# Four waits reordered, and the low parts of C and S moved from GpSimd to VectorE in three blocks of a hybrid decoder layer

## The reference

```
u, z, xbc, dt = split(rms_norm(h) @ w_in)
xbc = silu(causal_conv4(xbc));  x, B, C per group (4 groups, 6 heads of 64, state 128)
for each chunk of 128 positions, each group:
    y_diag = ((C B^T) * decay, causal) @ (x * dt)
    y_off  = (C @ S) * exp(a_cs)
    S      = S * exp(a_sum) + B^T @ (x * dt * decay_to_end)
    y      = rms_norm_group((y_diag + y_off + d_skip * x) * silu(z)) * ssm_norm_w
h = h + concat(pool_scale * (pooled(u) @ pool_w), y) @ w_out
h = h + relu(rms_norm(h) @ w_ff1)^2 @ w_ff2
```

## Time and profile before

| | |
|---|---|
| median of 3 runs | 2731.99 us (2728.07 to 2734.66) |
| profiled execution | 2732.35 us, its span 2730.6 us |
| TensorE busy | 2688.2 us, 98% |
| VectorE, ScalarE, GpSimd busy | 60%, 47%, 40% |
| mean granted clock of TensorE | 0.996 of 2.4 GHz |

### The profile page before, as it was taken

One profiled execution on the slowest core, in us unless ns is written; L12 is line 12 of the kernel. 1 busy time (PEld: TensorE's weight loads), 2 busy tenths in 40 slices (PEclk: granted clock), 3 DMA queues, 4 the chain that ended last, 5 costly groups with the idle time before them and its releaser, 6 DMA issues. The chain is left out here.

```text
span 2730.6 us, 37588 instructions
## 1 busy us (share of the span) xinstructions
PE 2688.2 (98%) x14034; PEld 2251.3 (82%) x14034; DVE 1629.4 (60%) x2193; ACT 1279.8 (47%) x2562; POOL 1078.9 (40%) x858
## 2 busy tenths in 40 slices
PE   8999999999999999999999999999999999999998
PEld 6788777988788987888988888888888888888887
DVE  3588722678426775158764466664444666666666
ACT  2476754557325665246642554554545322222323
POOL 1033331234101333013334588765555535353434
PEclk9999999999999999999999999999999999999999
DMA  9677586545556446555356546673444843333323
GB/s 292 214 264 251 188 289 239 211 175 189 214 199 236 153 176 228 206 224 187 147 211 242 177 162 228 246 277 131 167 144 175 329 155 107 140 110 137 116 93 154
DMA packets 225491, 531.14 MB, mean 195 GB/s; under 512 B 14090, under 2 KB 98062, under 8 KB 215838
## 3 DMA queue, kind: packets, MB, share of 16 engines
q1 hardware_dynamic: 225310, 528.74, 54.0%
HBM read 382.74 MB, written 145.95 MB: 194 GB/s over the span
## 5 line engine op out<-in xcount | busy, mean ns | idle before, releaser
L1785 PE MATMUL bank<-hnT_hi,w_ring 128*128 128x512 f32 x1152 | 369.3, 392 | 0.7 <-DMA w_ring<-w_scr 0.7
L2129 PE MATMUL bank<-w_first,T_hi 128*128 128x512 f32 x896 | 275.9, 389 | 0.1
L2248 DVE SCALAR_TENSOR_TENSOR acc<-pre,par,acc 128x512 f32<-128x512 f32 x240 | 212.0, 883 | 91.8 <-ACT pre L1304 85.9
L1785 PEld LDWEIGHTS bank<-hnT_hi,w_ring 128*128 128x128 f32 x1152 | 216.3, 188 | 45.4 <-issue 1.0
L2595 DVE TENSOR_TENSOR acc_th<-bank,acc_th 128x512 f32<-128x512 f32 x224 | 150.0, 686 | 155.9 <-PE bank L2129 155.7
L2097 PE MATMUL bank<-T_hi,w_both 128*128 128x512 f32 x768 | 242.2, 389 | 0.2 <-DVE ff L2536 0.2
L1829 PE MATMUL bank<-w_ring,T_hi 128*128 128x512 f32 x768 | 240.2, 394 | 0.0
L1785 PE MATMUL bank<-hnT_lo,w_ring 128*128 128x512 f32 x576 | 224.5, 390 | 0.0
L2129 PEld LDWEIGHTS bank<-w_first,T_hi 128*128 128x128 f32 x896 | 168.1, 188 | 35.4 <-issue 0.5
L1809 PE MATMUL bank<-w_ring,hnT_hi 128*128 128x384 f32 x768 | 195.9, 336 | 0.0
L1785 PE MATMUL bank<-hnT_hi,w_both 128*128 128x512 f32 x576 | 193.0, 407 | 2.1 <-DVE w_both L540 2.1
(11 more groups left out here) (308 smaller groups left out, 6234.9 us busy)
## 6 DMA issues: line engine op xcount, KB each, us to landing
w_ring<-w_scr SPq DMA_DIRECT2D x312, 512.0 KB, 4.2
T_scr<-stage SPq DMA_DIRECT2D x32, 1792.0 KB, 6.6
w_scr<-w_both SPq DMA_DIRECT2D x104, 512.0 KB, 4.0
pair_raw<-in_w_ff SPq DMA_DIRECT2D x36, 1024.0 KB, 5.5
third<-T_scr SPq DMA_DIRECT2D x28, 1024.0 KB, 4.9
pair_raw<-T_scr SPq DMA_DIRECT2D x28, 1024.0 KB, 4.8
sums<-sums_scr SPq DMA_DIRECT2D x64, 384.0 KB, 4.9
raw<-in_w_in SPq DMA_DIRECT2D x36, 512.0 KB, 5.9
```

Source lines behind the costliest of these rows:

```text
L1785: mm = nc.tensor.matmul(bank[s][:, :], w[:, k, :], t[:, k, :], start=(k == 0 and j == 0), stop=(k == KT - 1 and j == 2))
L2129: mm = nc.tensor.matmul(bank[4 * half + t][:, :], a[:, k, tok], w[:, k, :], start=(SECOND[q % 7] not in GOES_ON and k == 0 and j == 0), st ...
L2248: ins = nc.vector.scalar_tensor_tensor(acc[:, s, 0:TB], pre[:, s, k:k + TB], w, acc[:, s, 0:TB], ALU.mult, ALU.add)
```

## The change

1. **Output weights** (`scale_rows`, `high_part`): the scaling of unit N + 1 is done in the call of high_part(N), ahead of N's waits for the unit before and for the store (from unit 38 on; units 36 to 38 are scaled in their own call, now ahead of the other waits). The copies T_hi of the pool mixer move from u = 0, 1 to u = 1, 2.
2. **Sums' store**: in block 0 behind load(12) and no longer behind load(11).
3. **z of step 12**: in block 0 the three transposes of z, with their wait for the units, move from slot1 to behind the unit n2 and get a semaphore of their own; ScalarE's copy moves behind its evacuation of that unit; the mask waits for C B^T alone.
4. **Offset copies**: in steps 14 and 15 of every block, the finish of the pool unit moves behind yo.
5. **Low parts of C and S** in blocks 1 to 3: two subtractions leave GpSimd's queue and become `cs_low` in VectorE's, behind xw and ahead of y_low.

```diff
@@ -25,6 +25,7 @@
 KT = D_MODEL // P
 CONV_TILES = (D_SSM + 2 * GROUPS * P) // P
 STEPS = GROUPS * CH
+Z_LATE = STEPS - CH
 
 
 UNITS_G = 8
@@ -352,6 +353,7 @@
                        for c in range(CH)]
         xb_ps = sig("xb_ps", STEPS)
         zc_ps = sig("zc_ps", STEPS)
+        z_late = sem("z_late")
         xb_ready = sig("xb_ready", STEPS)
         exp_ready = sig("exp_ready", STEPS)
         zs_ready = sig("zs_ready", STEPS)
@@ -506,6 +508,9 @@
 
         def scale_rows(act, N):
 
+            if not U_OUT <= N < UNITS:
+                return
+            act.wait_ge(raw_ready[N % RING], 16 * (N // RING + 1 + (N % RING == 0)))
             if N in FOLDED:
                 f = FOLDED.index(N)
                 for kk in range(2):
@@ -523,9 +528,11 @@
 
             if N >= UNITS:
                 return
+            if U_OUT <= N <= U_OUT + 2:
+                scale_rows(act, N)
+            if N >= U_OUT + 2:
+                scale_rows(act, N + 1)
             act.wait_ge(raw_ready[N % RING], 16 * (N // RING + 1 + (N % RING == 0)))
-            if N >= U_OUT:
-                scale_rows(act, N)
             if N >= 2:
                 act.wait_ge(unit_done.sem, N - 1)
                 act.wait_ge(w_stored[N % 2], 32 * (N // 2))
@@ -794,7 +801,7 @@
                     N0 = b * UNITS
                     for n in range(RING, U_OUT):
                         load(N0 + n, in_unit(n))
-                        if n == (8 if b else 11):
+                        if n == (8 if b else 12):
                             store_sums(b)
                         if n == (8 if b else 12):
                             sums_stored.wait(sp, b, 16 * GROUPS)
@@ -1071,15 +1078,6 @@
                         if b and n == 0:
                             inverse_root(b - 1, r2[:, :], ssf[:, :], h_sumsq, CH, h_rstd, CH)
                     for q, g, c, n1, n2 in mixer_plan(b):
-                        if b:
-                            cs_split_hi.wait(pool, b, 2 * q + 1)
-                            nc.gpsimd.tensor_tensor(c_both[:, 1, :],
-                                                    group_tile(g, 1)[:, c * P:(c + 1) * P],
-                                                    c_both[:, 0, :].bitcast(F32), ALU.subtract)
-                            cs_split_hi.wait(pool, b, 2 * q + 2)
-                            nc.gpsimd.tensor_tensor(s_both[:, 1, :], S[:, g, :],
-                                                    s_both[:, 0, :].bitcast(F32), ALU.subtract
-                                                    ).then_inc(s_split_lo.sem, 1)
                         if q:
                             inverse_root(b, rsy[:, :], ssy[:, :], ssy_ready, q, rsy_ready, 1)
 
@@ -1391,6 +1389,15 @@
                     rsy_ready.wait(act, b, q + 1)
                     nc.scalar.activation(y[:, :], y[:, :], ACT.Copy, scale=rsy
                                          ).then_inc(yn_ready.sem, 1)
+
+                def z_copy(q):
+                    if q == Z_LATE:
+                        act.wait_ge(z_late, 1)
+                    else:
+                        zc_ps.wait(act, 0, q + 1)
+                    gated.wait(act, 0, q)
+                    nc.scalar.activation(zs[:, :], bank[3][:, 0:GW], ACT.Copy
+                                         ).then_inc(zs_ready.sem, 1)
 
                 def y_squares(b, q):
                     gated.wait(act, b, q + 1)
@@ -1483,11 +1490,8 @@
                                              ).then_inc(xb_ready.sem, 1)
                         if b and n1 is None:
                             s_high(b, q)
-                        if b == 0:
-                            zc_ps.wait(act, b, q + 1)
-                            gated.wait(act, b, q)
-                            nc.scalar.activation(zs[:, :], bank[3][:, 0:GW], ACT.Copy
-                                                 ).then_inc(zs_ready.sem, 1)
+                        if b == 0 and q != Z_LATE:
+                            z_copy(q)
                         if q:
                             y_squares(b, q - 1)
                         if q > 1:
@@ -1503,6 +1507,8 @@
                             high_part(act, N0 + n2[0] + 2)
                         for n in n2:
                             evac(b, n)
+                        if b == 0 and q == Z_LATE:
+                            z_copy(q)
                         pending = n2[-1]
                     y_squares(b, STEPS - 1)
                     y_high(b, STEPS - 2)
@@ -1513,8 +1519,8 @@
                             high_part(act, N0 + U_OUT + d * 8 + u + 2)
                             if d == 0 and u == 0:
                                 y_norm(b, STEPS - 1)
-                            if d == 0 and u < 2:
-                                for i in (2 * u, 2 * u + 1):
+                            if d == 0 and u in (1, 2):
+                                for i in (2 * u - 2, 2 * u - 1):
                                     up_out.wait(act, b, pool_item(b) + i + 1)
                                     nc.scalar.activation(T_hi[:, i, :], F[:, i * TB:(i + 1) * TB],
                                                          ACT.Copy).then_inc(pool_hi.sem, 1)
@@ -1849,6 +1855,17 @@
                                                  h[:, t, k * P:(k + 1) * P], ident[:, :])
                     mm.then_inc(hT_ps.sem, 1)
 
+                def z_transposes(q, g, c):
+
+                    zs_ready.wait(pe, 0, q)
+                    if c == 0:
+                        up_out.wait(pe, 0, (g + 1) * UNITS_G)
+                    for i in range(3):
+                        mm = nc.tensor.transpose(bank[3][:, i * P:(i + 1) * P],
+                                                 group_tile(g, 5 + i)[:, c * P:(c + 1) * P],
+                                                 ident[:, :])
+                    return mm
+
                 def slot1(b, q, g, c):
 
                     cols = slice(c * P, (c + 1) * P)
@@ -1865,13 +1882,8 @@
                                                  group_tile(g, j)[:, cols], ident[:, :])
                     mm.then_inc(xb_ps.sem, 1)
                     g_ready.wait(pe, b, q)
-                    if b == 0:
-                        zs_ready.wait(pe, b, q)
-                        if c == 0:
-                            up_out.wait(pe, b, (g + 1) * UNITS_G)
-                        for i in range(3):
-                            nc.tensor.transpose(bank[3][:, i * P:(i + 1) * P],
-                                                group_tile(g, 5 + i)[:, cols], ident[:, :])
+                    if b == 0 and q != Z_LATE:
+                        z_transposes(q, g, c)
                     nc.tensor.matmul(bank[3][:, GW:GW + P], group_tile(g, 0)[:, cols],
                                      group_tile(g, 1)[:, cols], start=True, stop=True
                                      ).then_inc(zc_ps.sem, 1)
@@ -2011,6 +2023,9 @@
                             state(b, q - 1)
                         for n in n2:
                             unit(b, n)
+                        if b == 0 and q == Z_LATE:
+                            g_ready.wait(pe, b, q + 1)
+                            z_transposes(q, g, c).then_inc(z_late, 1)
                         y_offset(b, q, g, c)
                     y_transposes(b, STEPS - 2)
                     diagonal(b, STEPS - 1)
@@ -2333,6 +2348,14 @@
                     scd_ready.wait(dve, b, q + 1)
                     nc.vector.tensor_tensor(S[:, g, :], bank[7][:, 0:GW], S[:, g, :], ALU.add
                                             ).then_inc(state_ready.sem, 1)
+
+                def cs_low(b, q, g, c):
+                    cs_split_hi.wait(dve, b, 2 * q + 2)
+                    nc.vector.tensor_tensor(c_both[:, 1, :], group_tile(g, 1)[:, c * P:(c + 1) * P],
+                                            c_both[:, 0, :].bitcast(F32), ALU.subtract)
+                    nc.vector.tensor_tensor(s_both[:, 1, :], S[:, g, :],
+                                            s_both[:, 0, :].bitcast(F32), ALU.subtract
+                                            ).then_inc(s_split_lo.sem, 1)
 
                 def xw_low(b, q):
                     xw_split_hi.wait(dve, b, q + 1)
@@ -2441,6 +2464,8 @@
                         nc.vector.tensor_tensor(by_head(xw[:, :]), by_head(xb[:, :]),
                                                 per_head(dtw, c, g), ALU.mult
                                                 ).then_inc(xw_ready.sem, 1)
+                        if b:
+                            cs_low(b, q, g, c)
                         if q > 1:
                             y_low(b, q - 2)
                         if b:
@@ -2448,15 +2473,14 @@
                         if c and n1 is not None:
                             finish(b, pending)
                         finish(b, n1)
-                        if n1 is None and c >= 2:
-                            finish(b, pending - 1)
-
                         yoff_ps.wait(dve, b, q + 1)
```

(2 more changed lines are left out.)

## The result

The changed kernel takes 2762.72 us (median of 4 runs, 2760.14 to 2764.26) and the kernel before, on the same chip, 2732.82 us (2728.07 to 2734.66). The ratio is 1.011, with a 95% interval of 1.0096 to 1.0123: slower by 29.9 us. The forecast was 2768.5 us with a range of 2746 to 2785. The profiled span is 2761.2 us against 2730.6.

A forecast was written before the change was run, and what follows sets the result against it. The prediction took TensorE's work plus its waits (busy 2688.2 of 2730.6 us) as the bound. From 2732.35 us, less 17.6 of gains, plus 44.6 of y_offset waits and 9.2 of slow clock: 2768.5 us, range 2746 to 2785.

The forecast's parts named there:

- The chain of 5.90 us: Blocks 1 to 3: uncontended time from the start of state_add through xw and the low parts to y_offset, 5.90 us.
- The sign that the taps take 2.3 us everywhere: VectorE's three taps: with GpSimd's subtraction gone they take 2.3 us everywhere in the new trace.
- The waits: Blocks 1 to 3: y_offset waits 1.13, 2.43 and 1.40 us in steps like 1, 2 and 4; 44.6 us in all.
- The meeting: GpSimd's ty meets VectorE's low-part subtractions: 0.5 us in steps like 1 and 2, 0.25 us in those like 4.
- The clock: Nine y_offset waits of about 2.4 us slow TensorE's clock, costing 9 x 0.6 x 1.7 = 9.2 us.
- The share of 0.6: The factor 0.6 applied to nine long y_offset waits, each slow-clock stretch costing 1.7 us.
- Block 0: Gains in block 0: sums' store 3.8 us, z of step 12 2.0 us, output weights 2.8 us.
- Offset copies: Steps 14 and 15: waits for yo go, net 8.8 - 3.2 = 5.6 us, plus 3.4 us of slow clock.
- Rival 1: Blocks 1 to 3: meetings with GpSimd cost nothing and the clock drops once at most; 2748 us, chance 0.20.
- Rival 2: Meetings cost 0.83 us in 18 steps, all nine long waits halve the clock, gains 14 us; 2785.6 us, chance 0.12.
- Rival 3: VectorE reaches cs_low in time, so the gains alone remain; 2714.8 us, chance 0.03.
- rival 4: The named stalls go but the costs happen to cancel them; 2732 us, chance 0.03.

The follow-up runs named there:

- e5: The changed kernel with GpSimd's product ty moved behind its carry in blocks 1 to 3: 2749.78 us.
- e3: The changed kernel with the subtractions of C and S ahead of the mask in steps 0 to 11, between xdt and xw in 12 to 15: 2714.88 us.
- e2: The kernel before with only the low parts of C and S moved to VectorE behind xw: 2778.77 us.
- e6: The kernel before with only the output weights' scaling and the pool copies T_hi moved: 2729.58 us.
- e7: The kernel before with only the sums' store moved one load later in block 0: 2730.53 us.
- e8: The kernel before with only the finish of the pool units moved behind yo in steps 14 and 15: 2724.38 us.
- e10: The kernel before with only the late z transposes of step 12 in block 0: 2728.78 us.
- e9: e3 with block 0's finish of the pool unit left ahead of yo in steps 14 and 15: 2715.49 us.
- e1: The changed kernel with the low parts of C and S back on GpSimd, so the four reorderings alone: 2716.56 us.
- e4: The changed kernel with the subtraction of S made twice in every step of blocks 1 to 3: 2802.81 us.

## Why the prediction was right

**The bound.** That the time is TensorE's work plus its waits held: 2690.7 us of work against 2688.2.

**The chain of 5.90 us.** It holds. In step 2 of block 1, state_add starts at 524.27 in the changed kernel and y_offset at 530.75, which is 6.48 us, where the prediction had 5.90 and 0.5 for the meeting. In e5, without a meeting, it is 528.76 - 522.92 = 5.84 us. The chain was right to 0.06 us, with 0.20 us (c_both, from 529.31 to 529.51) where I had estimated 0.24. The sign that the taps take 2.3 us everywhere holds for those in the chain, behind state_add (2.32 us). Later taps still take up to 2.95 us (at 502.51), beside GpSimd's ty + yo.

**The waits.** Predicted were 1.13, 2.43 and 1.40 us; the rows show 1.05, 2.34 and 0.98 with 1.19 in step 15, together 43.2 us, inside the 40 to 50 of the prediction. Where they fall is as predicted, in steps 3, 7, 11 to 14 too. A wait costs more than its row says, though: state(q) of steps 1, 2 and 4 is 1.33, 2.62 and 1.25 us later than the step before left it. TensorE's idle time is counted from the end of its last matmul, which takes 0.39 us while the next could start 0.22 us behind its start (0.17 us more), and y_offset itself takes 0.79 us behind a wait instead of 0.69. I had worked with starts, so the sum to compare is 14.9 us a block predicted (nine waits) with 3 x 1.33 + 3 x 2.62 + 2 x 1.25 = 14.35 us measured for eight of them, and step 0's 0.6 to 1.5 us on top.

**The meeting.** I took 0.5 us in the classes of steps 1 and 2 and 0.25 in that of step 4; it was 0.63 and about 0.1. The order in time shows what happens: ty ends at 530.28, S at 530.69, 0.41 us later; in e3 ty ends at 512.16 and xw at 512.57, 0.41 again. The second operation gets on only when the first is over. That is what the Trainium skill, SBUF — State Buffer, section "Who interferes with whom", says of the exclusive lock, and the trace agrees. By that page I had put the cost of a meeting at up to ty's whole 0.83 us; it is less, because 0.20 of ty's 0.97 us are over when S's turn comes (0.77 us are left), and S ends 0.41 us behind ty and not 0.55.

**The clock** is the term that was mis-sized: 9 x 0.6 x 1.7 = 9.2 us predicted, one stretch or 1.7 us measured, so 7.5 us too much, where the forecast is 5.8 us above 2762.72. The other terms miss too: by the table and with the clock taken out, block 0 and the last steps gave some 1.7 and 1.6 us more than predicted, steps 0 to 11 cost nearly 4 us more than 44.6, and the end 1.4. That these almost cancel is luck. The share of 0.6 is not what failed: behind the waits of this length of the kernel before (2.1 us for weights, 2.2 us for z, 2.3 us in step 15) the clock fell 14 times out of 25, in one profile each of the kernels that keep them (before, e2, e6, e7, e8, e10). What failed is carrying it over to waits at another place: behind y_offset's waits of 2.34 us it fell in one of nine here and in one of nine in e2, and never behind e5's 1.7 us.

**Block 0.** Predicted 3.8 + 2.0 + 2.8 = 8.6 us, measured 9.5. The sums' store and z alone are near the prediction (e7: 3.6, e10: 2.4). In the changed kernel the store gives 2.7 us up to y_offset(11), since a wait of 0.85 us for a later unit's weights (at 146.40) comes in, which I had put at nothing. For fold(41) I expected 2.7 us of waiting for the landing; e6 alone shows 1.65 + 0.44, and the changed kernel 0.84, since the landing came 24.5 us behind y_offset(15) and not 25.1, and since TensorE was held up by 1.41 and 0.89 us in step 15, which is the effect of the offset copies that I had not foreseen. With the finish behind yo, ScalarE's next evacuation waits 2.05 us for it (at 322.34), and what ScalarE feeds comes later, up to T_lo. It cost nothing (e9).

**Offset copies.** Predicted was 5.6 us net and 3.4 us of clock, 9.0; the table gives 3 x 2.4 = 7.2, and both slow stretches of before are gone, 3.4, together 10.6. Step 15's new wait was 1.19 us, not 1.05. But 0.4 us a block of waiting for y at the same place went too. Whether this clock time is the reordering's to save is not shown: in the profiled executions of e1 and e8 the clock fell behind the new, shorter waits, but these are among the slowest of their kernels. Why it stayed up in the changed kernel I can't say from these runs.

**The rivals.** Rival 1 (2748) had the clock right and the meetings wrong: e5, which takes the meetings away, has 2749.8 (and no slow clock). Rival 2 had the meetings near (0.63, not 0.83) and the clock wrong. Rival 3 (VectorE in time) and rival 4 are excluded by the waits of 1 and 2.3 us. The gains of 19.5 and 14 us in rivals 1 and 2 are given without their working; the table's gains are 9.5 + 10.6 = 20.1 us.

## What to carry to other kernels

An operation given to an engine with room (60% busy) costs what its place in that engine's queue makes it cost: the same two subtractions cost some 47 us behind xw (e2 against the kernel before) and nothing that shows ahead of the mask (e3 against e1). Before moving one, set the end of what stands ahead of it in the queue against the start of its consumer, step class by step class. And count a reordering's gain at the next thing that TensorE can't pass (here a DMA's landing), not at the wait that it removes.

## What the runs showed of the hardware

- An operation of VectorE with two SBUF sources that starts while one of GpSimd runs ends a fixed time behind it, however long it has waited: 0.41 us for 128x384 float32 (it then takes up to 1.18 us for 0.55), 0.55 us for 128x512 and 1.08 us for 128x1024, all in the changed kernel. If VectorE is first, GpSimd's is the one that grows: ty took 0.97 us beside c_both's 0.28, and 0.98 us in step 15, where S had started 0.26 us ahead of it and kept its 0.55.
- Behind waits of 2.1 to 2.4 us TensorE's clock halved in some cases and not in others: 14 times out of 25 behind the waits of this length that the kernel before has, but for 3.4 us behind one of nine waits of 2.34 us in the changed kernel, and behind six of nine of 2.93 us in e4. It also fell behind 0.5 and 1.2 us with 0.8 us of work between them, in three blocks of three in e1's profile and in two of three in e8's. A mean wait is a poor guide to this cost, and a share read at one place doesn't carry over to another; what decides in a single case stays open.
- The same 2.33 us waits of step 15, in kernels that leave them untouched, halved the clock for 3.4 us, for 6.8 us or not at all (before, e7), so a sum of some us on the clock can't be had from one profile.
